# Up-projections of an MLP: products accumulated onto copies of other products in PSUM, the copies made by ScalarE, in place of sums on VectorE

## The reference

```python
h2 = rms_norm(x, norm2_g)                                              # 1024 x 1024
u = square(relu(einsum('bsd,df->bsf', h2, w_mlp_in)))                   # 1024 x 4096
x = x + einsum('bsf,fd->bsd', u, w_mlp_out)                             # 1024 x 1024
```

## Time and profile before

| | us |
|---|---|
| median of 3 runs | 1274.12 (1273.73 to 1274.68) |
| the profiled execution's own time | 1274.64 |
| its span, first to last instruction | 1272.7 |
| TensorE busy | 1243.1 (98%) |
| VectorE busy | 960.1 (75%) |
| ScalarE busy | 560.9 (44%) |
| up-projection on TensorE | 656.42 to 963.26, 306.84 long |
| down-projection on TensorE | 963.26 to about 1268.8 |

### The profile page before, as it was taken

One profiled execution on the slowest core, in us unless ns is written; L12 is line 12 of the kernel. 1 busy time (PEld: TensorE's weight loads), 2 busy tenths in 40 slices (PEclk: granted clock), 3 DMA queues, 4 the chain that ended last, 5 costly groups with the idle time before them and its releaser, 6 DMA issues. The chain is left out here.

```text
span 1272.7 us, 17523 instructions
## 1 busy us (share of the span) xinstructions
PE 1243.1 (98%) x6057; PEld 1044.0 (82%) x6057; DVE 960.1 (75%) x1442; ACT 560.9 (44%) x981; POOL 163.1 (13%) x293
## 2 busy tenths in 40 slices
PE   5999999999989999999999999999999999999998
PEld 5888888887878888888887888888888888888887
DVE  5877776778987769773588787787778898879864
ACT  5656555656543423322245554454454433333330
POOL 2424323333100031000000000000000000000034
PEclk9999999999999999999999999999999999999999
DMA  8010010100455465532213534534559644363333
GB/s 262 24 51 18 25 42 0 49 16 17 154 169 174 153 220 180 184 116 97 85 67 132 174 121 164 171 123 164 168 192 352 258 160 171 99 227 105 99 97 134
DMA packets 111816, 165.97 MB, mean 130 GB/s; under 512 B 5357, under 2 KB 59266, under 8 KB 111746
## 3 DMA queue, kind: packets, MB, share of 16 engines
q1 hardware_dynamic: 111746, 165.05, 38.3%
HBM read 116.80 MB, written 48.23 MB: 130 GB/s over the span
## 5 line engine op out<-in xcount | busy, mean ns | idle before, releaser
L2152 PE MATMUL bank<-o_hi,s_hi 128*128 128x512 f32 x448 | 174.4, 389 | 0.6 <-DVE s_lo L2005 0.6
L2152 PE MATMUL bank<-o_hi,s_lo 128*128 128x512 f32 x448 | 174.3, 389 | 0.0
L2152 PE MATMUL bank<-slot_hi,featT_hi 128*128 128x384 f32 (+1 forms) x320 | 117.7, 368 | 4.8 <-DVE slot_lo L1376 3.0
L2152 PE MATMUL bank<-slot_lo,featT_hi 128*128 128x384 f32 (+1 forms) x320 | 111.7, 349 | 0.0
L2152 PE MATMUL bank<-slot_hi,featT_lo 128*128 128x384 f32 (+1 forms) x320 | 111.5, 348 | 0.0
L2061 DVE TENSOR_TENSOR c<-bank,c 128x512 f32<-128x512 f32 x112 | 75.7, 688 | 35.0 <-PE bank L2152 33.4
L2152 PE MATMUL bank<-featT_hi,pair_hi 128*128 128x512 f32 x256 | 99.9, 390 | 0.8 <-DVE c L2061 0.8
L2152 PE MATMUL bank<-featT_lo,pair_hi 128*128 128x512 f32 x256 | 99.6, 389 | 0.0
L2152 PE MATMUL bank<-featT_hi,pair_lo 128*128 128x512 f32 x256 | 99.6, 389 | 0.0
L2152 PE MATMUL bank<-o_lo,s_hi 128*128 128x512 f32 x256 | 99.6, 389 | 0.0
L2152 PEld LDWEIGHTS bank<-o_hi,s_hi 128*128 128x128 f32 x448 | 84.1, 188 | 18.5 <-DVE s_lo L2005 1.0
(11 more groups left out here) (250 smaller groups left out, 3160.8 us busy)
## 6 DMA issues: line engine op xcount, KB each, us to landing
s_raw<-u_store SPq DMA_DIRECT2D x28, 1024.0 KB, 5.5
pair_raw<-in_w_mlp_in SPq DMA_DIRECT2D x16, 1024.0 KB, 5.9
u_store<-s_tile SPq DMA_DIRECT2D x64, 256.0 KB, 2.1
o_raw<-in_w_mlp_out SPq DMA_DIRECT2D x16, 1024.0 KB, 7.8
u_store<-u_tile SPq DMA_DIRECT2D x48, 256.0 KB, 2.4
gate_store<-out_tile SPq DMA_DIRECT2D x32, 256.0 KB, 2.1
gate_raw<-in_w_in SPq DMA_DIRECT2D x8, 1024.0 KB, 5.5
raw<-in_w_in SPq DMA_DIRECT2D x15, 512.0 KB, 4.5
```

Of the source, the lines that this page charges most:

```text
L2152: mm = nc.tensor.matmul(out, a, b, start=start and i == 0, stop=stop and i == len(steps) - 1)
```

## The change

TensorE makes the same products with the same operands, in another order, and many of them go on top of what a bank already holds. "Seeding" a bank is a ScalarE copy from one bank to another (`seed_bank`).

- P2 accumulates onto the bank of P1: this is c11, with no add.
- ScalarE copies the bank of P1 to a second bank, and P6 accumulates onto the copy. For p > 0 ScalarE copies that one (P1 + P6) to a third bank, and P7 accumulates onto it. P3 accumulates onto the bank of P1 + P6.
- In pairs 2 to 14, P4 accumulates onto the bank of P7, once VectorE has read it for c22.
- ScalarE copies P5 to SBUF (`keep_p5`); in pairs 0, 1 and 15 it also copies the bank of P6 or P7 (`keep_u`).
- The adds on VectorE fall from 7 to 2 for each pair (`SUMS`: 4 in pair 0, 3 in pairs 1 and 15). Relu reads c11, and in pairs 2 to 14 c21, from PSUM.
- The order of a pair becomes P1, P5, P6, P2, P7, P3, P4; that of pair 15 P5, P1, P4, P6, P2, P7, P3. The first two pairs are interleaved as `FIRST_PAIRS` says, and the orders of the splits on ScalarE and VectorE, the waits and the orders of the stores on SP follow.

The diff, cut to its core:

```diff
+        P5, P4, P1, P6, P2, P7, P3 = range(7)
+        FIRST_PAIRS = ((0, P5), (0, P4), (1, P5), (1, P4), (0, P1), (1, P1), (0, P6), (0, P7), (0, P2), (0, P3), (1, P6),
+                       (1, P2), (1, P7), (1, P3))
+        def up_order(p):
+            return (P5, P1, P4, P6, P2, P7, P3) if p == PAIRS - 1 else (P1, P5, P6, P2, P7, P3, P4)
         def turn(p, i):
 
+            return FIRST_PAIRS.index((p, i)) + 1 if p < 2 else 7 * p + up_order(p).index(i) + 1
...
+        def up_banks(p):
             if p == 0:
...
+                return {P1: 2, P2: 2, P6: 3, P3: 3, P7: 4, P5: 6, P4: 1}
+            a, b, e, g = (4, 3, 0, 6) if p % 2 == 0 else (5, 1, 2, 7)
+            h = {1: 0, PAIRS - 1: 4}.get(p, e)
+            return {P1: a, P2: a, P6: b, P3: b, P7: e, P5: g, P4: h}
+        SUMS = [4] + [3] + [2] * (PAIRS - 3) + [3]
+        def sums_before(p):
+            return sum(SUMS[:p])
+        def c22_sum(p):
+            return sums_before(p) + (3 if p == 0 else 1)
+        def c12_sum(p):
+            return sums_before(p + 1)
+        def has_c21_sum(p):
+            return SUMS[p] > 2
+        def seed(p, second=False):
+            return 1 if p == 0 else 2 * p + second
...
+            t_split_hi(0, P1)
+            t_split_hi(1, P1)
+            t_split_hi(0, P6)
+            h2_split_hi(T - 1)
+            for i in (P7, P2, P3):
                 t_split_hi(0, i)
-            h2_split_hi(T - 1)
-            for i in (P7, P3):
-                t_split_hi(0, i)
...
+            def seed_bank(p, second):
+                b = up_banks(p)
+                src, dst = (b[P6], b[P7]) if second else (b[P1], b[P6])
+                act.wait_ge(p_done, turn(p, P6 if second else P1))
+                if p == 0:
+                    act.wait_ge(res_ready, 2 * T)
+                elif p == 1:
+                    if second:
+                        act.wait_ge(relu_done, 1)
+                    else:
+                        act.wait_ge(up_sum, 2)
+                elif not second:
+                    act.wait_ge(up_sum, c12_sum(p - 2))
+                elif p < 4:
+                    act.wait_ge(up_sum, sums_before(1) + 2)
+                    act.wait_ge(u_kept, 2)
+                else:
+                    act.wait_ge(relu_done, 4 * (p - 2) + 4)
+                nc.scalar.activation(bank[:, dst, :], bank[:, src, :], ACT.Copy).then_inc(seeded, 1)
+            def keep_p5(p):
+                act.wait_ge(p_done, turn(p, P5))
+                if p > 1:
+                    act.wait_ge(up_sum, c12_sum(p - 2))
+                nc.scalar.activation(kept5[p % 2][:], bank[:, up_banks(p)[P5], :], ACT.Copy).then_inc(p5_kept, 1)
+            def keep_u(p):
+                act.wait_ge(p_done, turn(p, P6 if p == 0 else P7))
+                if p == 0:
+                    act.wait_ge(res_out[0], 48)
+                else:
+                    act.wait_ge(u_ready, 4 * (p - 1) + 4)
+                    act.wait_ge(up_sum, c22_sum(p))
+                nc.scalar.activation(c21[:], bank[:, up_banks(p)[P6 if p == 0 else P7], :], ACT.Copy).then_inc(u_kept, 1)
...
+                n = (0, 3, 1, 2)[i]
                 c = (c11, c21, c22, c12)[i]
-                act.wait_ge(up_sum, 7 * p + (3, 5, 6, 7)[i])
-                nc.scalar.activation(c[:], c[:], ACT.Relu).then_inc(relu_done, 1)
-                act.wait_ge(relu_done, 4 * p + i + 1)
+                src = c[:]
+                if i == 0:
+                    act.wait_ge(p_done, turn(p, P2))
+                    src = bank[:, up_banks(p)[P2], :]
+                elif i == 1 and has_c21_sum(p):
+                    act.wait_ge(up_sum, sums_before(p) + 2)
+                elif i == 1:
+                    act.wait_ge(p_done, turn(p, P4))
+                    src = bank[:, up_banks(p)[P4], :]
+                else:
+                    act.wait_ge(up_sum, c22_sum(p) if i == 2 else c12_sum(p))
+                if p == 0:
+                    act.wait_ge(res_out[0], 48)
+                else:
+                    act.wait_ge(u_ready, 4 * (p - 1) + n + 1)
+                nc.scalar.activation(c[:], src, ACT.Relu).then_inc(relu_done, 1)
+                act.wait_ge(relu_done, 4 * p + n + 1)
...
+            keep_p5(0)
+            keep_p5(1)
             for p in range(PAIRS):
-                more = p + 1 < PAIRS
-                if more:
-                    for i in range(2 if p == 0 else 0, 5):
-                        t_split_hi(p + 1, i)
-                else:
+                if p == PAIRS - 1:
+                    keep_p5(p)
+                seed_bank(p, False)
+                if 1 < p < PAIRS - 1:
+                    keep_p5(p)
+                if p == 0:
+                    keep_u(p)
+                next_hi(p, 0, 1, 2)
+                if p == PAIRS - 1:
                     down_hi(0)
...
+                if p > 0:
+                    seed_bank(p, True)
+                next_hi(p, 3)
                 relu_square(p, 0)
-                if more:
-                    t_split_hi(p + 1, 5)
-                    t_split_hi(p + 1, 6)
-                else:
+                if p == PAIRS - 1:
                     down_hi(1)
+                next_hi(p, 4)
+                if p in (1, PAIRS - 1):
+                    keep_u(p)
+                relu_square(p, 2)
+                next_hi(p, 5)
+                relu_square(p, 3)
+                next_hi(p, 6)
                 relu_square(p, 1)
-                relu_square(p, 2)
-                relu_square(p, 3)
...
-                    dve.wait_ge(p_done, turn(p - 2, P3))
+                    dve.wait_ge(p_done, turn(p - 2, out))
...
-                dve.wait_ge(u_ready, 4 * p + 2)
+                dve.wait_ge(u_ready, 4 * p + 4)
...
             for p in range(PAIRS):
-                more = p + 1 < PAIRS
-                p5, p4, p1, p6, p2, p7, p3 = (bank[:, product_bank(p, i), :] for i in range(7))
+                b = {i: bank[:, n, :] for i, n in up_banks(p).items()}
+                n = sums_before(p)
                 if p == 0:
                     t_sum(1, 3)
-                    for i in range(2, 5):
-                        t_split_lo(1, i)
-                elif more:
+                elif p + 1 < PAIRS:
                     t_sums(p + 1)
-                    for i in range(5):
-                        t_split_lo(p + 1, i)
+                next_lo(p, 0, 1)
                 if p > 0:
                     u_sums(p - 1)
-                if not more:
+                next_lo(p, 2, 3)
+                if p == PAIRS - 1:
                     down_lo_o(0)
                     down_lo_s(0)
-                def up_add(i, out, psum, other):
-                    nc.vector.tensor_tensor(out[:], psum, other[:], ALU.add).then_inc(up_sum, 1)
...
+                dve.wait_ge(p_done, turn(p, P7))
+                p5 = kept5[p % 2][:]
+                dve.wait_ge(p5_kept, p + 1)
                 if p == 0:
-                    dve.wait_ge(res_out[0], 48)
-                else:
-                    dve.wait_ge(relu_done, 4 * (p - 1) + 4)
-                    dve.wait_ge(u_ready, 4 * (p - 1) + 4)
-                up_add(1, c21, p6, c11)
-                dve.wait_ge(up_sum, 7 * p + 1)
-                if p == 0:
-                    dve.wait_ge(res_out[1], 48)
-                up_add(2, c12, p5, c21)
-                dve.wait_ge(p_done, turn(p, P2))
-                up_add(3, c11, p2, c11)
-                if more:
-                    t_split_lo(p + 1, 5)
-                    t_split_lo(p + 1, 6)
-                dve.wait_ge(p_done, turn(p, P7))
-                up_add(4, c22, p7, c21)
-                dve.wait_ge(up_sum, 7 * p + 4)
-                up_add(5, c21, p4, c22)
-                dve.wait_ge(up_sum, 7 * p + 5)
-                up_add(6, c22, p5, c22)
+                    dve.wait_ge(u_kept, 1)
+                    up_add(p, c22, b[P7], c21[:], 5)
+                    dve.wait_ge(up_sum, 1)
+                    up_add(p, c21, b[P4], c22[:], 4)
+                    dve.wait_ge(up_sum, 2)
+                    up_add(p, c22, p5, c22[:], 5)
+                else:
+                    up_add(p, c22, b[P7], p5, 5)
+                    if has_c21_sum(p):
+                        dve.wait_ge(u_kept, 2 if p == 1 else 3)
+                        up_add(p, c21, b[P4], c21[:], 4)
+                next_lo(p, 4)
                 dve.wait_ge(p_done, turn(p, P3))
-                up_add(7, c12, p3, c12)
+                up_add(p, c12, b[P6], p5, 6)
+                next_lo(p, 5, 6)
...
                 if p == 0:
...
+                    if i == P4:
+                        pe.wait_ge(res_ready, 2 * T - 2)
+                    elif i == P1:
+                        pe.wait_ge(res_ready, 2 * T - 1)
+                    elif i == P7:
                         pe.wait_ge(h2_f, 16)
                     elif i == P3:
-                        pe.wait_ge(first_copied, 1)
...
+                        pe.wait_ge(u_kept, 1)
+                elif i == P1:
```

(80 more changed lines are left out.)

47 lines of the change are left out of this document (12 added, 35 removed).

## The result

The changed kernel takes 1279.88 us (median of 5 runs, 1278.59 to 1280.46), against 1274.12 before: 1.0044 of it, with a 95% interval from 1.0033 to 1.0056. It is slower by 5.8 us; the forecast was 1279.4. The profiled execution took 1280.46 us, 5.8 more than that of before.

A forecast was written before the change was run, and what follows sets the result against it. TensorE, busy for 98% of the span, was taken as the bound. Waits won back -1.3, first pause 0.85, second 4.1 and clock 1.6 sum to +5.25 us, giving 1279.4 us from the median; range 1277.3 to 1282.2 us.

The forecast's parts named there:

- That TensorE can win at most 1.3 us: Up-projection: relieving VectorE returns at most 1.3 us, chiefly TensorE's two waits for adds in pairs 0 and 1.
- The distance of matmuls: Up-projection: matmuls start 0.227 us apart beside idle or busy engines alike, so no gain there.
- The price of a seed: ScalarE's copy from bank to bank: 0.58 us taken from nearest rows, with ends of 0.4 and 1.2 us.
- The first pause: Near 674 us, TensorE waits 0.75 us for pair 0's seed before (0,P6), and loses 0.1 us behind it.
- The second: About 685 to 689 us, TensorE waits 4.0 us for pair 1's seed before (1,P6), plus 0.1 us behind it.
- The clock: Behind the 4.0 us pause, granted clock falls to half for 3.4 us, costing 1.6 us; ends 0 and 3.2.
- The end: Pair 15: last sum of squares 0.7 us later; product 3's load still in time, nothing counted, up to 1.5 us if late.
- The tightest seed: Pair 2: its seed ends 0.9 us before (2,P6) wants it, so no wait there.
- The pauses, but the clock stays: Rival: both pauses occur in the first pairs but the clock stays full, 1277.8 us; chance 0.22.
- The second pause isn't there: Rival: ScalarE's work between (0,P3) and the seed of (1,P6) doesn't hold it up, 1273.7 us; chance 0.08.
- A slow copy: Rival: bank-to-bank copies beside TensorE's writes take 1.2 us, adding 0.6 to each pause, 1280.6 us; chance 0.07.
- matmuls closer together: Rival: matmuls come closer when VectorE reads PSUM less; at 6 ns each over 1344 matmuls, 1271.5 us; chance 0.02.

The follow-up runs named there:

- both pauses mended: Changed kernel with pair 1's first seed behind relu_square(0, 0), pair 0's seed ahead of both P5 copies, pair 1's second seed ahead of three splits: 1273.13 us.
- the one moved instruction: Changed kernel with the seed of pair 1 placed behind relu_square(0, 0) on ScalarE, not behind all of turn p = 0: 1273.65 us.
- the kernel with 18 filling matmuls: Changed kernel plus 18 matmuls with unused results on TensorE between (0,P3) and (1,P6): 1279.41 us, repeated 1279.02 us.
- the kernel filled with 12 matmuls: Changed kernel plus 12 matmuls with unused results on TensorE between (0,P3) and (1,P6): 1278.07 us.
- the one of 2.8: Changed kernel with the seed of pair 1 behind relu_square(0, 3) and ahead of relu_square(0, 1) on ScalarE: 1278.27 us.
- filled with 6: Changed kernel plus 6 matmuls with unused results on TensorE between (0,P3) and (1,P6): 1278.39 us.

## Why the prediction was right

*That TensorE can win at most 1.3 us* (the stage's length less its matmuls): right. The kernel with both pauses mended won 1.0 in its profile, with 0.3 still lost at (2,P6).

*The distance of matmuls*: right, 0.227 us before and after, with 50 us less work on VectorE.

*The price of a seed*, 0.58 us by the nearest rows, between 0.4 and 1.2: it measured 0.58 us in 30 of the 31 seeds and 0.60 in one. The Trainium skill, "ScalarE: Activation LUTs" (Step-by-step), has PSUM as ScalarE's faster destination; a copy from PSUM to SBUF took 0.60 us here. So the trace agrees with the direction, but the difference is 0.02 us and moves nothing.

*The first pause*, 0.75 us: 0.71. *The second*, 4.0 us by the hand-overs, an add, two relus, two squares and a seed: 4.03. That the place in the queue decides it is shown by the one moved instruction. The hand-over from ScalarE to TensorE was estimated at 0.1 us; the seed ended at 688.88, TensorE started at 689.03, 0.15.

*The clock*: that it falls was right, the size short. I counted one fall for 3.4 us, 1.6 us; in both profiles it lasted 6.8, of which 5.3 and 6.2 us fell on matmuls and cost 2.5 and 2.9 us. So the term that was mis-sized is the fall's length; the upper end of 3.2 us was nearer than the value taken. The other runs may have had a shorter one: the mean granted clock was 0.996 to 0.998 in the five runs of its first measurement, and the profiled run, with 0.996, was the slowest of them. The other three terms, -1.2 + 0.8 + 4.0 = 3.6, are 3.65 in the forecast. With 2.5 the stage is 6.1 us longer in the profile; the whole execution is 5.8 us longer, as the stage began 0.3 us earlier (656.10 against 656.42), and so are the medians, 0.5 more than the 5.25 forecast. The rule of the Trainium skill, "TensorE: Matmul & The Clock Gate" (Part 1), that idleness brings the throttled clock back, agrees with the trace: 4.0 us of standing still and half clock, the same time filled with work and full clock.

*The end.* The last sum of squares comes 0.5 us later behind the start of the down-projection than before (979.04 - 969.04 against 972.78 - 963.26), and 0.7 was expected; the split for product 3 ends at 999.96, 1.7 us ahead of its product. No cost, as forecast. The risk of a late load was real, as the kernel with 18 filling matmuls shows, but sat at product 5 and not at product 3.

*The tightest seed*, 0.9 us to spare in pair 2: right for this kernel, 1.0, and 1.0 with the pause filled too. But part of it comes of the pauses: without the second 0.7 us are left, and with both mended the seed is 0.2 us late. The spare time of a seed belongs to one order of work, and has to be worked out again when a pause ahead of it goes.

*The rivals.* "The pauses, but the clock stays" would be 1277.8; the kernel filled with 12 matmuls, which comes nearest to it, took 1278.1. "The second pause isn't there" is 1273.7, and the kernel with the seed moved took 1273.65. A slow copy is ruled out by its 0.58 us, matmuls closer together by their 0.227, and a late load for product 3 by its split, 1.7 us ahead. One slip: at 6 ns for each matmul the sum is 1279.4 - 8.1 = 1271.3, not 1271.5.

## What to carry to other kernels

When an engine's queue is strict, moving work to an engine with time to spare costs nothing only if that engine's program comes to it in time: ask of each step that a busy engine waits for what stands ahead of it in its queue, and what the last of these waits for, above all in prologues, where the steady order isn't reached yet. Taking work off an engine gives back at most what the bound engine lost waiting for it, here 1.3 us of 1274; that number is to be read first. And a pause of TensorE can be dearer than its length: the one of 4.0 us cost 6.5 in the first profile, the one of 2.8 cost 4.4, while those of 0.7 and 1.3 cost 0.1 more than they lasted.

## What the runs showed of the hardware that I had not expected

The granted clock's fall about a pause isn't fixed by the pause's length. A stand-still of 2.8 us was followed by half clock for 3.4 us, one of 2.65 by none in its profile, one of 4.0 went with 6.8 us twice. (The idle time in the rows' brackets is shorter than the stand-still that the starts give: 2.69, 2.50 and 3.87 us.) The same pause near 356 us, 3.3 to 3.6 us by its brackets, had 3.4 us at half in most profiles, 6.8 in one, and none in two (one seed moved; filled with 6). Nor is the moment of the fall fixed: 2.5 us into the pause of 4.0 in the first profile of the changed kernel, 3.4 us into it in the second, and 0.7 us behind the end of the pause of 2.8. Busy time by stretch near 356 us, without a fall and with the long one:

```profile
356.00:361.00 5.00, 4.12 (x18) 3.43 (x19) 5.00 (x7) 4.14 (x6) 0.00 (x0) 1.00 0.28 105
```

```profile
357.38:362.76 5.38, 5.38 (x13) 4.22 (x14) 5.38 (x6) 5.38 (x8) 0.00 (x0) 0.50 0.26 97
```

The first is of the kernel filled with 6 matmuls, the second of the changed kernel's second profile, from the first matmul behind the pause to the end of half clock. So part of the spread from run to run can be the clock's: near 356 us a fall of 3.4 us cost 1.6 us against none, and the long one, which began within the pause, 0.9 us more.
